# Three transformer blocks on one core: the two norms between block 1 and block 2 taken from one weighted sum of squares, and the first norm's own mean computed later

## What is computed

```python
# end of the first block (its second half is an MLP with a causal convolution)
x = x + (jax.nn.silu(a) * bgate) @ w_down[l]
return rmsnorm(x, final_norm_g)
...
# start of the second block: its own norm, then the input projection
y = x32 * lax.rsqrt(jnp.mean(x32 * x32, axis=-1, keepdims=True) + EPS)
return (y * g.astype(jnp.float32)).astype(x.dtype)
```

## Time and profile before

| what | us |
|---|---|
| median of 3 runs | 3049.65 (3046.66 to 3049.84) |
| the profiled execution, its own time | 3054.0 |
| its span | 3052.7 |
| PE / DVE / ACT busy | 2899.6 / 1926.3 / 1295.3 |
| down phase at the seam, first matmul to last | 1145.8 to 1167.5 |
| the means on PE | 1172.5 to 1182.6 |
| the pair on PE | 1188.5 to 1212.3 |
| key projection on PE | 1212.3 to 1223.3 |

### The profile page before, as it was taken

One profiled execution on the slowest core, in us unless ns is written; L12 is line 12 of the kernel. 1 busy time (PEld: TensorE's weight loads), 2 busy tenths in 40 slices (PEclk: granted clock), 3 DMA queues, 4 the chain that ended last, 5 costly groups with the idle time before them and its releaser, 6 DMA issues.

```text
span 3052.7 us, 35598 instructions
## 1 busy us (share of the span) xinstructions
PE 2899.6 (95%) x14338; PEld 2243.9 (74%) x14338; DVE 1926.3 (63%) x2829; ACT 1295.3 (42%) x2024; POOL 0.4 (0%) x5
## 2 busy tenths in 40 slices
PE   8999799999999998999999989999898999999997
PEld 7787587788888875777775767665566888888884
DVE  5543338777777678676784664667666755555556
ACT  4223415434443445454546454555643433233323
POOL 0000000000000000000000000000000000000000
PEclk9999899999999998999999999999989999999998
DMA  4211111111111111111010111000001111111111
GB/s 155 75 55 45 32 42 39 51 49 54 44 63 49 56 49 42 35 42 42 28 36 27 42 35 35 22 17 27 28 21 35 42 55 62 49 56 47 58 49 69
DMA packets 48833, 141.72 MB, mean 46 GB/s; under 512 B 12790, under 2 KB 16670, under 8 KB 48542
## 3 DMA queue, kind: packets, MB, share of 16 engines
q1 hardware_dynamic: 48670, 139.45, 14.6%
HBM read 135.16 MB, written 9.77 MB: 47 GB/s over the span
## 4 chain that ended last, share of the span: by engine, by line
PE 80%; DVE 10%; ACT 6%; issue 4%; DMA 0%; DVEq 0%; SPq 0%; ACTq 0%
PE psum L848 24%; PE psum L529 16%; PE psum L888 14%; PE psum L1076 10%; PE psum L562 4%; PE psum L626 2%; PE psum L1158 1%; PE psum L1185 1%; DVE residual L2243 1%; PE psum L1013 1%; PE psum L992 1%; PE psum L676 1%; DVE mlp_ta L2531 1%; PE psum L621 1%; DVE residual L2646 1%
## 5 line engine op out<-in xcount | busy, mean ns | idle before, releaser
L2180 ACT ACTIVATE w_hi<-w_raw 128x512 fp32r<-128x512 f32 x288 | 179.9, 625 | 318.9 <-DVE w_raw L3295 194.1
L2646 DVE TENSOR_TENSOR residual<-residual,psum 128x1024 f32<-128x1024 f32 x176 | 213.9, 1220 | 139.7 <-PE psum L888 139.5
L848 PE MATMUL psum<-h_hi,w_hi 128*128 128x512 f32 x640 | 249.1, 389 | 0.1
L848 PE MATMUL psum<-h_hi,w_lo 128*128 128x512 f32 x640 | 249.0, 389 | 0.0
L848 PE MATMUL psum<-h_lo,w_hi 128*128 128x512 f32 x640 | 248.9, 389 | 0.0
L529 PE MATMUL psum<-h_hi,w_hi 128*128 128x512 f32 x752 | 237.8, 397 | 7.9 <-DVE w_lo L2228 3.3
L888 PE MATMUL psum<-mlp_act_hi,w_hi 128*128 128x512 f32 x704 | 220.8, 395 | 14.8 <-DVE residual L2646 9.2
L529 PE MATMUL psum<-h_hi,w_lo 128*128 128x512 f32 x752 | 232.0, 390 | 0.0
L529 PE MATMUL psum<-h_lo,w_hi 128*128 128x512 f32 x752 | 231.9, 389 | 0.0
L3318 DVE TENSOR_TENSOR w_lo<-w_raw,w_hi 128x512 fp32r<-128x512 f32 x288 | 197.7, 687 | 38.3 <-ACT w_hi L2180 38.2
L888 PE MATMUL psum<-mlp_act_hi,w_lo 128*128 128x512 f32 x704 | 218.7, 392 | 0.0
(11 more groups left out here) (415 smaller groups left out, 5442.8 us busy)
## 6 DMA issues: line engine op xcount, KB each, us to landing
w_raw<-in_weights SPq DMA_DIRECT2D x228, 512.0 KB, 3.6
residual<-in_x_t SPq DMA_DIRECT2D x8, 512.0 KB, 8.6
out_t<-residual SPq DMA_DIRECT2D x8, 512.0 KB, 3.0
rel_copies<-rel_rows SPq DMA_DIRECT2D x8, 480.0 KB, 5.7
na_bias<-rel_copies SPq DMA_DIRECT2D x8, 240.0 KB, 4.5
band_copies<-band_rows SPq DMA_DIRECT2D x8, 192.0 KB, 6.1
ret_rotary<-in_rotary SPq DMA_DIRECT2D x1, 1024.0 KB, 11.9
swa_bias<-band_copies SPq DMA_DIRECT2D x4, 256.0 KB, 2.8
```

The lines of the kernel that those rows point to most:

```text
L848: ins = self.pe.matmul(out[bank[j]], w[:, k, :], x(k), start=(j in emptied and k == 0 and part == 0), stop=(k == 3 and part == 2), skip_gr ...
L2180: self.act.activation(dst, m.block_source(plan, n), ACT.Copy).then_inc(*self.to("mw_hi_" + name, n))
L2646: self.dve.tensor_tensor(x, x, self.m.place["down", t, n], ALU.add).then_inc(*self.to("dve_down", t, n))
```

## The change

The weighted squares alone are summed in the down phase, with the weight root = sqrt(g3^2 + eps), so that one mean gives the whole n4 factor. Root and eps^2 are made ahead of the MLP. The last of the 8 tiles and everything behind it up to the first normalised tile goes by token halves. The mean adds the last two tiles of squares on PE instead of on DVE. The n3 squares are taken after all eight normalised tiles, on ACT and DVE, their mean on PE between the pair and the key projection, its Ln and Exp on ACT ahead of na_queries(0).

```diff
+        self.gains, self.root = at("norm34_gains", 54784, [P, KD]), at("norm34_root", 54816, [P, KD])
+        self.eps_n4 = at("norm34_eps", 54848, [P, 1])
...
+    def last_second_halves(self, plan, g):
+
+        t, n = plan.d[2 * g + 1], 3
+        m, block = self.m, plan.first["down", g] + 2 + n // 2
+        out = self.wide(("down", t, n), ("dve_down", t, n))
+        self.q.wait_ge(*self.on("mw_lo_" + plan.name, block))
+        w_hi, w_lo = (m.block(buf, block).rearrange("p (k n) -> p k n", k=2)[:, :, P:2 * P] for buf in (m.w_hi, m.w_lo))
+        for half, s in halves():
+            for k in range(2):
+                for part, (w, x) in enumerate(((w_hi, m.act_hi), (w_lo, m.act_hi), (w_hi, m.act_lo))):
+                    ins = self.pe.matmul(out[:, s], w[:, k, :], x[:, k, s], start=(k == 0 and part == 0), stop=(k == 1 and part == 2))
+            ins.then_inc(*self.to("down", t, n, *upto(half)))
...
     def means_after_mlp1(self):
+
-        out3 = self.acc(("pe_n3_mean",), ("act_n3_rstd", 1))
-        q.wait_ge(*on("dve_n3_acc", KD - 2))
-        q.wait_ge(*on("act_n3_sq", KD - 1))
-        self.sum_of(out3, "mean1024", (m.n_acc, m.n_buf1), "pe_n3_mean")
-        out4 = self.acc(("pe_n4_mean",), ("dve_n4_mean", 1))
-        q.wait_ge(*on("dve_n4_acc", KD - 2))
-        q.wait_ge(*on("act_n4_sq", KD - 1))
-        self.sum_of(out4, "mean1024", (m.m_acc, m.m_buf1), "pe_n4_mean")
+        out = self.acc(("pe_n4_mean",), ("act_n4_rstd", 1))
+        for half, s in halves():
+            q.wait_ge(*on("dve_n4_acc", KD - 3))
+            self.pe.matmul(out[:, s], m.c("mean1024"), m.n_acc[:, s], start=True, stop=False)
+            q.wait_ge(*on("act_n4_sq", KD - 2))
+            self.pe.matmul(out[:, s], m.c("mean1024"), m.n_buf0[:, s], start=False, stop=False)
+            q.wait_ge(*on("act_n4_sq", KD - 1, *upto(half)))
+            self.pe.matmul(out[:, s], m.c("mean1024"), m.n_buf1[:, s], start=False, stop=True).then_inc(
+                *self.to("pe_n4_mean", half))
+
+    def n3_mean(self):
+
+        self.q.wait_ge(*self.on("dve_n3_acc", KD - 1))
+        out = self.take(("pe_n3_mean",), 6, 2, ("act_n3_rstd", 1))
+        self.sum_of(out, "mean1024", (self.m.m_acc,), "pe_n3_mean")
...
+    def project_pair_first(self, name, emptied0, emptied1):
...
+        out = [self.acc(("proj", t), emptied0), self.acc(("proj", t + 1), emptied1)]
+        order = [(0, j, (h,)) for h in range(2) for j in range(2)]
+        order += [(n, j, range(2)) for n in range(1, KD - 3) for j in range(2)] + [(n, j, range(2)) for j in range(2) for n in range(KD - 3, KD)]
+        for k, j, hs in order:
...
-        self.project_pair(lambda k: ("act_n4_hi", k), lambda k: ("dve_n4_lo", k), ("act_nq", 0), ("act_nv", 0))
+        self.project_pair_first("n4", ("act_nq", 0), ("act_nv", 0))
+        self.n3_mean()
         self.project(("act_nk", 0))
...
-    def both_squares(self, k):
+        q.wait_ge(*on("dve_gains"))
+        self.act.activation(m.root[:], m.root[:], ACT.Ln, bias=m.c(f"eps{EPS}", 1)).then_inc(*self.to("act_root_ln"))
+        q.wait_ge(*on("act_root_ln"))
+        self.act.activation(m.root[:], m.root[:], ACT.Exp, scale=0.5).then_inc(*self.to("act_root"))
+
+    def n4_square(self, k):
...
+                        if k == 1:
+                            q.wait_ge(*on("act_root"))
+                            self.act.preload_act_table_set("natural_log_exp_and_others")
                         if k:
-                            self.both_squares(k - 1)
-        self.both_squares(KD - 1)
-        self.next_split = plan.base + 66
+                            self.n4_square(k - 1)
+                        if k == 6:
+                            self.next_split = plan.base + 66
+                            self.split_up_to(B2)
+        last = KD - 1
+        for half in range(2):
+            q.wait_ge(*on("dve_down", plan.d[2 * NGROUP - 1], 3, *upto(half)))
+            self.half_square("n4", half, last, m.root[:, last:KD])
...
+        def rstd(half):
+            s = slice(half * HALF, half * HALF + HALF)
+            self.act.activation(m.n_rstd[:, s], m.place[("pe_n4_mean",)][:, s], ACT.Ln, bias=m.eps_n4[:]).then_inc(
...
+        rstd(0)
         self.split_up_to(B2 + 1)
-        self.rsqrt(m.place[("pe_n3_mean",)], m.n_rstd, EPS, ("pe_n3_mean",), ("act_n3_rstd",))
-        for half, s in halves():
-            q.wait_ge(*on("dve_n4_mean", half))
-            act.activation(m.m_rstd[:, s], m.m_rstd[:, s], ACT.Ln, bias=m.c(f"eps{EPS}", 1)).then_inc(*to("act_n4_ln", half))
-            q.wait_ge(*on("act_n4_ln", half))
-            act.activation(m.m_rstd[:, s], m.m_rstd[:, s], ACT.Exp, scale=-0.5).then_inc(*to("act_n4_rstd", half))
-        self.high_parts("n4", (m.m_buf0, m.m_buf1))
+        high(0)
+        rstd(1)
+        high(1)
+        for k in range(1, KD):
+            q.wait_ge(*on("dve_n4_scaled", k))
+            self.act.activation(m.h_hi[:, k, :], (m.m_acc, m.m_buf0, m.m_buf1)[k % 3][:], ACT.Copy).then_inc(
+                *self.to("act_n4_hi", k))
+        for k in range(KD):
+            if k < 3:
+                q.wait_ge(*on("dve_n4_lo", KD - 1))
+            self.squares("n3", k, m.x[:, k, :])
...
+        self.rsqrt(m.place[("pe_n3_mean",)], m.m_rstd, EPS, ("pe_n3_mean",), ("act_n3_rstd",), True)
         self.na_queries(0)
...
+        g3, g4 = (m.vec[:, VEC[name]:VEC[name] + KD] for name in ("final_norm_g", "ln_g_2"))
+        self.dve.memset(m.eps_n4[:], EPS * EPS)
+        self.dve.tensor_tensor(m.root[:], g3, g3, ALU.mult)
+        self.dve.tensor_tensor(m.gains[:], g3, g4, ALU.mult).then_inc(*self.to("dve_gains"))
...
                 for o in (2 * j, 2 * j + 1):
                     half = (c - plan.base) % 2
-                    self.add_down(c, half, o)
                     k = 4 * half + o
-                    if last and k:
-                        self.add_squares("n3", k - 1, m.n_acc, (m.n_buf0, m.n_buf1))
-                        self.add_squares("n4", k - 1, m.m_acc, (m.m_buf0, m.m_buf1))
+                    if last and 2 <= k < KD - 1:
+                        self.add_squares("n4", k - 1, m.n_acc, (m.n_buf0, m.n_buf1))
+                    if last and k == KD - 1:
+                        self.half_down(c, o, 0)
+                        self.half_down(c, o, 1)
+                    else:
+                        self.add_down(c, half, o)
+                    if last and k == KD - 2:
+                        self.next_split = plan.base + 66
+                        self.split_up_to(B2)
             if ahead:
...
+        first(0)
         self.split_up_to(B2 + 1)
-        self.combine("n4", "act_n3_rstd", ("pe_n4_mean",))
-        self.after("dve_gains")
-        self.split_norm("n4", (m.m_buf0, m.m_buf1), m.m_rstd, lambda k: m.gains[:, k:k + 1], "dve_n4_rstd")
+        first_low(0)
+        first(1)
+        first_low(1)
+        for k in range(1, KD + 1):
+            if k < KD:
+                if k == 3:
+                    self.after("dve_n4_lo", 0, 1)
+                elif k > 3:
+                    self.after("dve_n4_lo", k - 3)
+                self.scale(bufs[k % 3], m.x[:, k, :], m.gains[:, k:k + 1], m.n_rstd, ("dve_n4_scaled", k))
+            if k > 1:
+                self.low(k - 1, bufs[(k - 1) % 3][:], m.h_hi[:, k - 1, :], "act_n4_hi", "dve_n4_lo")
+        for k in range(KD):
+            self.add_squares("n3", k, m.m_acc, (m.m_buf0, m.m_buf1))
...
-        self.split_up_to(B2 + 2)
+        self.split_up_to(B2 + 3)
+        q.wait_ge(*on("act_n3_rstd", 1))
         for k in range(KD):
-            self.scale(m.x[:, k, :], m.x[:, k, :], m.v("final_norm_g", k), m.n_rstd, ("dve_n3_applied", k))
-            if k == 3:
-                self.split_up_to(B2 + 3)
+            self.scale(m.x[:, k, :], m.x[:, k, :], m.v("final_norm_g", k), m.m_rstd, ("dve_n3_applied", k))
         self.after("dve_n3_applied", KD - 1)
```

More of the change, by code:

```diff
@@ L875, in last_second @@
         t = plan.d[2 * g + 1]
-        for n in range(4):
+        for n in range(3 if plan is PLAN1 else 4):
             out = self.wide(("down", t, n), ("dve_down", t, n))
@@ new lines, in n3_mean @@
+    def n3_mean(self):
[3 more added lines that the diff above has]
+    def project_pair_first(self, name, emptied0, emptied1):
+        t = self.tile
+        self.q.wait_ge(*self.on("w_lo", t))
+        out = [self.acc(("proj", t), emptied0), self.acc(("proj", t + 1), emptied1)]
+        order = [(0, j, (h,)) for h in range(2) for j in range(2)]
+        order += [(n, j, range(2)) for n in range(1, KD - 3) for j in range(2)] + [(n, j, range(2)) for j in range(2) for n in range(KD - 3, KD)]
+        for k, j, hs in order:
+            self.q.wait_ge(*self.on("w_lo", t + j))
+            w_hi, w_lo = self.weights(t + j)
+            at = hs if k == 0 else ()
+            for part, (w, low) in enumerate(((w_hi, 0), (w_lo, 0), (w_hi, 1))):
+                if part == 0:
```

(35 more changed lines are left out.)

32 lines of the change are left out of this document (25 added, 7 removed).

## The result

The changed kernel takes 3055.06 us (median of 17 runs, 3053.07 to 3057.43) against 3049.63 of the kernel before (17 runs beside it): a ratio of 1.0019, interval 1.0013 to 1.0026. That is 5.4 us by the medians and 5.8 by the ratio; the forecast was 3055.8, 6.2 us above. The change makes the kernel slower, by an amount just inside the 0.2% that the prediction set as its bound: of its three outcomes it is "within", which had 0.43, and not "slower by more", which had 0.49.

The account below looks back on a forecast made before the run. PE, busy 95% of the span, bounds the kernel, so only the key projection's start and speed count: 3049.65 + 4.0 (later start) + 2.2 (lower clock) = 3055.8 us, range 3049.5 to 3060.0.

Parts of the forecast that it names:

- Down phase: Down phase ahead of n4's mean: round trip of addition, square and sum takes 3.62 us per tile, losing 0.2 per tile.
- Mean and factor: n4's mean and factor by halves: mean at full level, 0.86 us per part on one half; Ln and Exp 1.35.
- Normalised tiles: n4's tiles on DVE ahead of the pair: 2.46 us each, with three buffers as with two.
- End of the pair: Pair of projections on PE ahead of the key projection: ends at 1202.6 instead of 1212.28, 9.7 us earlier.
- (a) to (d): Between pair and key projection: n3's squares and sums, mean, factor, then queries' eviction; projection starts at 1216.3, +4.0 us.
- (e): Key projection: starting after a gap of 4.1 us costs it clock, +2.2 us.
- rival B: n3's mean and key projection: clock soon full again, mean 0.86 per half, projection loses only 1.6; 3053.0 us, chance 0.27.
- Edits at nothing: Root and gains ahead of the MLP, table load, scaling of x, first weight splits: all hidden, costing nothing.
- Rival A: Pair to key projection: n3's steps run in the pair's shadow, its 9.7 us lead kept; 3040.0 us, chance 0.09.
- Rival D: Token halves ahead of the pair: they bring PE nothing; already in the sum, no chance of its own.

Follow-up runs that it names:

- warm: Changed kernel plus products of a constant that nobody reads on TensorE, 9 ahead of the mean of n3 and 8 behind it; 3055.66 us.
- queries_first: Changed kernel with key projection ahead of n3's mean on TensorE, queries' eviction ahead of n3's factor but behind all eight squares on ScalarE; 3055.16 us.
- warm2: Changed kernel plus products of a constant that nobody reads on TensorE, 6 ahead of the mean of n3 and 5 behind it; 3053.76 us.
- keys_first: Changed kernel with key projection ahead of n3's mean on TensorE, queries' eviction between n3's second and third squares on ScalarE; 3041.50 us.
- best: both, plus n4's mean in banks 4 and 5, weight splits earlier, queries' eviction behind n3's first square; 3036.69 us, again 3037.85.
- both: keys_first, plus the down-phase sum put behind the addition on VectorE; 3039.65 us, again 3037.59.

## Why the prediction was right

Right in size and, for nearly every step, in place. That the total came out within 1 us (6.2 forecast, 5.4 by the medians, 5.8 by the ratio) is in part luck, since the interval alone is 2 us to either side; what bears the mechanism out are the steps. Positions of the forecast are moved by the 2.38 us between the two traces.

- **Down phase.** Additions 3.62 us apart forecast, 3.65 measured; the last half addition ends at 1170.6 forecast, 1170.69 measured; last product 1169.0 both. TensorE's wait of 3.9 us is 3.98, and it does fall to the low level behind it (0.76 over the phase, against 0.87 in the earlier trace rows) without being late. That the low level there costs nothing can be seen in warm and queries_first, where it begins about 1.5 us later behind the same wait:

```profile
1161.64 0.73 PE L905 MATMUL psum<-mlp_act_hi,w_hi 128*128 128x512 f32 x2 [4.07 <-DVE residual L2749]
```

  The last product starts 0.6 and 0.7 us earlier in these two, and the pair starts 32.8 us behind the first product all the same.
- **Mean and factor.** Half 1 of the mean at 1174.4 forecast, 1174.6 measured, at the full level; the scaling of the second tile at 1178.1, measured 1178.20; start of the pair 1176.1, measured 1176.21.
- **Normalised tiles.** 2.46 us per tile was too much: with three buffers the scalings are 2.33 apart. The last low part ends at 1194.71, not 1195.2. I had reasoned that a third buffer changes nothing. With two, a scaling starts 1.25 us behind the low part ahead of it (1190.89 to 1192.14 in the earlier trace rows), with three 1.13 (1182.95 to 1184.08); it then has a buffer whose last reader was done long before. No run has the third buffer as its only change.
- **End of the pair.** 1200.2 forecast, 1200.31 measured.
- **(a) to (d).** ScalarE's and VectorE's rows for these steps:

```profile
1196.85 8.79 DVE L2523 TENSOR_TENSOR norm_acc<-norm_acc,norm_buf 128x1024 f32<-128x1024 f32 x7 [2.14 <-ACT norm_buf L1455]
...
1209.51 0.69 ACT L1323 ACTIVATE norm_rstd<-psum,common 128x512 f32<-128x512 f32 x1 [0.36 <-PE psum L954]
1210.23 0.63 ACT L1326 ACTIVATE norm_rstd<-norm_rstd 128x512 f32<-128x512 f32 x1
1210.76 2.75 ACT L1802 ACTIVATE na_q<-psum,na_bq 64x512 f32<-64x512 f32 x4
```

  The sums end at 1205.64 (1206.1 forecast), 1.25 us each as taken; the mean runs low and ends at 1209.5 (1209.8); the factor ends at 1210.86 (1211.2); the key projection starts at 1213.66 (1213.9). +4.0 forecast, +3.8 measured.
- **(e)** was the term most off: 2.2 taken, 1.6 measured, the size that rival B gave it (B's other half, the mean at the full level, did not come). I had called the new gap near that of the pair, and that was a misreading: the pair's was 5.96 us, the one ahead of the down phase 3.87, and the new one, 4.19, is nearest to the latter, which had the higher price, 2.9. So the length of a gap doesn't rank these prices, and what does is not shown. warm2 confirms that the gap is the cause.
- **Edits at nothing.** Scaling of x ends at 1226.4 (1226.6 forecast), and no idle time of TensorE follows from it.

Rival A, the pair's lead kept, is what keys_first made of the kernel, but at a lower worth than A's 9.7 us: 6.7 below the kernel before by the ratio, 7.6 in the seam. The key projection does start 9.4 us earlier (57.11 against 66.51); A's sum left out that the mean of n3 still takes TensorE 1.7 us, now behind it. The condition given for it, that (a) to (d) lie in the shadow of the pair, was too strict. They need only stay off the path of the projection; what has to be done by the pair's end is the eviction of the queries and a weight split. Rival D was wrong where it said that the halves bring TensorE nothing: they bring the second tile 2.1 us earlier, and the pair's end 2.4.

## What to carry to other kernels

A chain that is shortened ahead of the busiest engine pays only if nothing that stood in its shadow now stands between that engine's next two jobs: list, for the next job, every buffer and operand that it waits for, and what stands ahead of those in their queues. Work whose result is needed later (here the mean for the residual) goes behind what the busiest engine waits for, on every engine it touches; moving only its mean and its factor gave 0.6 us by the runs (2.1 in the seam), letting what TensorE waits for past the squares too gave 12.5 (13.1). And taking instructions from the pacing engine gained nothing here, since the same edit put a consumer ahead of the next producer: look at the round trip, not at the sum.

## What the runs showed of the hardware

- Work whose result nobody reads, put into idle time of 5.4 and 4.2 us, kept TensorE's granted clock at 1.00, and made the seam 3.1 us shorter (2.1 by the runs, not clear of their intervals). Too much of it (warm: 18 and 16 records in place of 12 and 10) made the seam 1.05 us longer.
- A product of f32 constants 128x512 leaves two records of 0.43 us, 0.87 in all (warm: 18 records in 7.89 us); a matmul of the split (fp32r) weights leaves one at 0.23, both at the full level.
- Low stretches come in one execution and not in the next at the same place of the same instructions (0.89 and 1.00 between 1985 and 2000). Two medians of five runs differed by 3 us for kernels that then came out alike; that this was such stretches is likely but not shown, though the mean clock of the whole execution was 0.983 in three of best's five runs and 0.980 or 0.981 in all of both's.
- The price of the low level behind a wait isn't set by the wait's length alone: 2.9 us behind 3.87 (down phase before), 1.6 behind 5.96 (pair before) and 1.6 behind 4.19 (key projection after).
